# A convolution stage with eight row buffers, and weight sums moved from its first part into its second

## The reference, cut to what matters

```python
b_g, c_g, v = jnp.split(rmsnorm_and_modulate(x) @ w_in, 3, axis=-1)   # w_in: 1024 x 3072
u = c_g * v
z = causal_conv3_per_channel(u, conv_w)        # taps j = 0, 1, 2
out = (b_g * z) @ w_out                        # then x + (1 + g1) * out, norm, router, experts
```

## Time and profile before

| | us |
|---|---|
| median of 3 runs | 6204.08 (6202.45 to 6206.72) |
| the profiled execution's own time | 6206.02 |
| its span, first to last instruction | 6204.3 |
| conv front: PE's first and last product | 3204.0 to 3535.6 |
| conv second part: PE's first and last product | 3535.6 to 4233.1 |

### The profile page before, as it was taken

The page is one execution under the profiler, slowest core; times in us unless marked ns, Lnnn a source line. Parts: engine busy times, 40 slices in busy tenths (PEclk is TensorE's granted clock), DMA queues, the critical chain, the costliest instruction groups (busy, mean ns, idle before and its releaser), DMA issues. The chain is left out here.

```text
span 6204.3 us, 82965 instructions
## 1 busy us (share of the span) xinstructions
PE 5864.6 (95%) x28274; PEld 4784.7 (77%) x28275; DVE 3805.1 (61%) x5360; ACT 2134.5 (34%) x3188; POOL 2024.4 (33%) x1866
## 2 busy tenths in 40 slices
PE   7999989999899999999979999998997999999994
PEld 5876668888678888888867788887775888888884
DVE  6889945554455545555535588876776454556555
ACT  2334432222244334434334323321113333444434
POOL 6555538860122223222225500000112222222222
PEclk9999999999899999999989999999998999999997
DMA  4665664442267666777557845544445656777767
GB/s 152 176 189 153 191 222 151 139 137 82 105 213 214 195 179 196 220 209 220 156 152 268 290 145 182 185 148 160 154 156 186 192 170 174 216 219 238 214 201 282
DMA packets 620014, 1152.41 MB, mean 186 GB/s; under 512 B 121940, under 2 KB 218804, under 8 KB 618809
## 3 DMA queue, kind: packets, MB, share of 16 engines
q1 hardware_dynamic: 422256, 799.04, 38.0%
q0 software_dynamic: 92896, 315.82, 18.9%
q10 hardware_dynamic: 104682, 35.19, 2.2%
HBM read 863.32 MB, written 286.29 MB: 185 GB/s over the span
## 5 line engine op out<-in xcount | busy, mean ns | idle before, releaser
L2279 DVE SCALAR_TENSOR_TENSOR m_o<-m_pO,m_weight_of,m_gate 128x512 f32<-128x512 f32 x316 | 234.2, 746 | 711.3 <-PE m_pO L2022 397.3
L2246 DVE TENSOR_TENSOR m_w_lo<-m_w_raw,m_w_hi 128x1024 fp32r<-128x1024 f32 x512 | 596.1, 1214 | 0.1
L1906 POOL COPY m_gather_now<-m_gather_of 128x1 int32 (+1 forms) x161 | 181.6, 1128 | 1155.3 <-DMA x<-m_o,m_scatter_now 929.5
L2077 ACT ACTIVATE m_xT_hi<-m_pX 128x512 fp32r<-128x512 f32 x320 | 191.4, 599 | 999.8 <-PE m_pB L141 994.3
L139 PE MATMUL m_pA<-m_w_lo,m_xT_hi 128*128 128x512 f32 x1280 | 517.4, 404 | 14.7 <-DVE m_xT_lo L2257 14.7
L2065 ACT ACTIVATE m_w_hi<-m_w_raw 128x1024 fp32r<-128x1024 f32 x512 | 505.6, 1053 | 50.2 <-DMA m_w_raw<-in_moe_w_dram 28.9
L2018 PE MATMUL m_pO<-m_w_lo,m_hT_hi 128*128 128x512 f32 x1280 | 513.5, 401 | 0.4 <-ACT m_hT_hi L2082 0.2
L141 PE MATMUL m_pA<-m_w_hi,m_xT_hi 128*128 128x512 f32 x1280 | 503.3, 393 | 0.0
L140 PE MATMUL m_pA<-m_w_hi,m_xT_lo 128*128 128x512 f32 x1280 | 500.5, 391 | 0.0
L2018 PE MATMUL m_pO<-m_w_hi,m_hT_hi 128*128 128x512 f32 x1280 | 499.4, 390 | 0.0
L139 PE MATMUL m_pB<-m_w_lo,m_xT_hi 128*128 128x512 f32 x1280 | 498.1, 389 | 0.0
(11 more groups left out here) (524 smaller groups left out, 13561.0 us busy)
## 6 DMA issues: line engine op xcount, KB each, us to landing
m_w_raw<-in_moe_w_dram SPq DMA_DIRECT2D x384, 1024.0 KB, 7.2
conv_op_raw<-xr SPq DMA_DIRECT2D x84, 1024.0 KB, 5.2
glu_ada<-in_ada_w_dram POOLq DMA_DIRECT2D x96, 256.0 KB, 3.2
a_x<-in_x_dram SPq DMA_DIRECT2D x32, 512.0 KB, 3.6
a_ada<-in_ada_w_dram POOLq DMA_DIRECT2D x64, 256.0 KB, 3.5
s_u<-u SPq DMA_DIRECT2D x64, 256.0 KB, 2.7
s_r<-k SPq DMA_DIRECT2D x64, 256.0 KB
glu_x<-in_x_dram SPq DMA_DIRECT2D x32, 512.0 KB
```

The lines of the kernel that those rows point to most:

```text
L1906: pool.tensor_copy(gx[:], gidx[:, bass.ds(t, 1)]).then_inc(gi_ready, 1)
L2077: act.activation(xT_hi[:, 4 * q:4 * q + 4, :], pX[:, 4 * q:4 * q + 4, :], ACT.Copy).then_inc(xt_hi, 1)
L2246: tt(W13[s][1][:, m, k:k + 2, :], W13[s][0][:, m, k:k + 2, :], W13[s][2][:, m, k:k + 2, :].bitcast(F32), ALU.subtract).then_inc(w13_lo, 1)
L2279: dve.scalar_tensor_tensor(out=ob[:, n, :], in0=pO[:, n, :], scalar=wslot[:, bass.ds(tile_, 1)], in1=gate2[:, n, :], op0=ALU.mult, op1=ALU ...
```

## The change

- Eight row buffers. SP loads blocks 0 and 1 at once, and block b + 2 when block b has been turned. `std_of` of block b + 2 now stands at the head of ACT's round b, and `scaled` of block b + 2 in DVE's round b ahead of `taps_of(b, 1)`.
- POOL makes only the weight sums of quarter 1 in the front (two in block 0, one each in blocks 1 and 2). Those of quarters 2 and 3 become 24 small steps of 128 x 128 instructions (`small_mix`), two DMAs in and one out each, run in groups 0 to 2 and 4 to 6 of the second part: two ahead of a group's first stores of z and two behind them.
- The waits for the mix room move to the first instruction that writes each 8 KB of it: `keep` of operation 0 on ACT (tile 2), operations 1 and 3 on DVE (tiles 0 and 1). The places of `kept`, `vs`, `bs` change accordingly.
- Rows 4 to 6 take the place that weight 2 had, so weight 2 moves to a place that quarter 0's weights hold until the front's last product. SP loads it then, ahead of operand 2, and its split follows block 7.
- Low parts for `cout`: 0 between two sums of operation 81, 1 after it, 2 to 4 after 82, none after 83. The last three (`LATE_LOWS`) are made in `cout`, first of all on DVE, and PE waits for each at its first use.

```diff
-        mixes = [(MIXED, c, kk) for c in range(1, CHUNKS) for kk in range(KH)]
+        mixes = [(MIXED, 1, kk) for kk in range(KH)]
...
-            for _ in range(1 if b else 5):
+            for _ in range(2 if b == 0 else 1 if b < 3 else 0):
                 self.steps.append(mixes.pop(0))
...
+        self.small = [(c, kk, j) for c in range(2, CHUNKS) for kk in range(KH) for j in range(3)]
...
-        w_at = (48, 60, 136, 0, 12, 24, 36)
+        w_at = (48, 60, 12, 0, 24, 136, 36)
...
+        def all_mixed(eng, s):
+            eng.wait_ge(mix_st[s], 16 * len(range(s, len(seven.steps), TILES_)))
...
-                if kind == MIXED:
+                if kind == MIXED and c == 1:
                     mixed(sp, MIXED, c)
+                elif kind == MIXED:
+                    for q in range(2):
+                        sp.wait_ge(small_st[q], 16 * 3 * KH // 2 * (c - 1))
...
-            for j in range(TPB):
+            for j in range(2 * TPB):
                 sp.dma_start(rows[j][:], x_view[j]).then_inc(n_ld[j], 16)
...
-                if b + 1 < TB:
+                if b + 2 < TB:
                     sp.wait_ge(t_psum, KD * (b + 1))
                     for j in range(TPB):
-                        sp.dma_start(rows[j][:], x_view[TPB * (b + 1) + j]).then_inc(n_ld[j], 16)
+                        s = TPB * (b % 2) + j
+                        sp.dma_start(rows[s][:], x_view[TPB * (b + 2) + j]).then_inc(n_ld[s], 16)
...
-            for r in range(3):
+            for r in range(2):
                 weights(1, r)
...
             sp.wait_ge(mm, GROUPS * TB)
+            weights(1, 2)
             operand(2)
             weights(1, 3)
...
+                else:
+                    all_mixed(act, 2)
                 act.activation(kept[0][JS[i]][:], bank(n, JS[i])[:], ACT.Copy).then_inc(copied, 1)
...
             for b in range(TB):
+                if b + 2 < TB:
+                    for n in range(TPB * (b + 2), TPB * (b + 3)):
+                        std_of(n)
                 c_copy(b, 0)
...
-                if b + 2 < TB:
-                    for n in range(TPB * (b + 2), TPB * (b + 3)):
-                        std_of(n)
-            for s in range(TILES_):
-                act.wait_ge(mix_st[s], 16 * len(range(s, len(seven.steps), TILES_)))
+            w_high(1, 2)
...
-                ks = {OPS - 3: range(0, 3), OPS - 2: range(3, 6), OPS - 1: range(6, KD)}.get(n, ())
+                ks = {OPS - 3: range(0, 6), OPS - 2: range(6, KD)}.get(n, ())
...
+            def small_mix(i):
+                cc, kk, j = seven.small[i]
+                s, tt = i % 2, pool.tensor_tensor
+                if i + 1 < len(seven.small):
+                    small_fetch(i + 1)
+                pool.wait_ge(small_ld[s], 32 * (i // 2) + 32)
+                a11, a21, a12, a22 = (small[s][:, h, m * P:(m + 1) * P] for h in range(2) for m in range(2))
+                c(tt(a22, a21, a22, ALU.add))
+                c(tt(a21, a11, a21, ALU.subtract))
+                c(tt(a11, a22, a11, ALU.subtract))
+                c(tt(a12, a12, a11, ALU.subtract))
+                pool.dma_start(ws_dram[cc - 1, kk][:, :, j, :], small[s][:]).then_inc(small_st[s], 16)
...
             for n in range(TPB, 2 * TPB):
-                dve.wait_ge(t_psum, KD)
                 scaled(n)
...
-                taps_of(b, b % 2, 1, q(1))
-                gated(b, 1)
                 if b + 2 < TB:
                     for n in range(TPB * (b + 2), TPB * (b + 3)):
                         scaled(n)
+                taps_of(b, b % 2, 1, q(1))
+                gated(b, 1)
+            w_low(1, 2)
...
+                if n == 1:
+                    all_mixed(dve, 0)
+                if n == 3:
+                    all_mixed(dve, 1)
...
+                    if n == OPS - 3:
+                        next_low(0)
...
+            for k in range(KD if glu else KD - LATE_LOWS, KD):
+                dve.tensor_tensor(w_lo[:, k, :], w_raw[:, k, :], w_hi[:, k, :].bitcast(F32), ALU.subtract).then_inc(w_split, 1)
             dve.tensor_tensor(select[:], ident[:, 0:NL], ident[:, 64:64 + NL], ALU.add).then_inc(sel_set, 1)
```

More of the change, by code:

```diff
@@ L44 @@
 NG, EG, NE = 4, 8, 32
+KH = KD // 2
+SUPER = T // (2 * HALF)
+CHUNKS = 4
+SEVEN = 7
+LATE_LOWS = 3
 FE = 512
@@ L1280, in project @@
             _, here = core.sb_at(ctx, f"{tag}_w", [P, 22, D])
-            w_lo, w_hi, there, first_lo, first_hi = ready
+            w_raw, w_lo, w_hi, there, first_lo, first_hi = ready
             assert here == there
@@ L1669, in products @@
                             pe.wait_ge(w_split, (place * KD + k) // KQ + 1)
+                        if not glu and isinstance(i, int) and i + s + place == 0 and k >= KD - LATE_LOWS:
+                            pe.wait_ge(w_split, k - (KD - LATE_LOWS) + 1)
                         last = product(pe, pM[s][:, b, :], (h_hi[s][:, k, :], h_lo[s][:, k, :]),
@@ L2478, in conv_in @@
         w0_raw, w0_lo, w0_hi = first_w
-        rows = [at_(f"rows{j}", 48 + 4 * j, [P, D]) for j in range(TPB)]
+        last_row, last_row_at = core.sb_at(ctx, f"{tag}_rows7", [P, D])
+        rows = [at_(f"rows{j}", 48 + 4 * j, [P, D]) for j in range(TPB)] + [at_(f"rows{TPB + j}", 136 + 4 * j, [P, D]) for j in range(3)] + [last_row]
+        small = [nc.alloc_sbuf_tensor_at(f"{tag}_small{n}", [P, 2, W], F32, offset=last_row_at + 2 * KBYTES * n) for n in range(2)]
         junk = at_("junk", 64, [P, D])
@@ L2689, in turned @@
                 for j in range(TPB):
-                    last = pe.transpose(pT[n % 2][:, j * P:(j + 1) * P], rows[j][:, k * P:(k + 1) * P], ident[:])
+                    last = pe.transpose(pT[n % 2][:, j * P:(j + 1) * P], rows[TPB * (b % 2) + j][:, k * P:(k + 1) * P], ident[:])
                 last.then_inc(t_psum, 1)
@@ L2816, in store, with small_fetch @@
                 pool.dma_start(z_view[MC * (1 + g // SUPER) + m][2 * (g % SUPER) + t], z[q][:]).then_inc(y_st[q], 16)
-            for g in range(OPS // SEVEN):
-                store(g, 0)
-                store(g, 1)
+            def small_fetch(i):
+                cc, kk, j = seven.small[i]
+                s = i % 2
+                if i >= 2:
+                    pool.wait_ge(small_st[s], 16 * (i // 2))
+                for h in range(2):
+                    pool.dma_start(small[s][:, h, :], w_view[cc][:, KH * h + kk, j, :]).then_inc(small_ld[s], 16)
+            def small_mix(i):
+                cc, kk, j = seven.small[i]
+                s, tt = i % 2, pool.tensor_tensor
[8 more added lines that the diff above has]
+                pool.dma_start(ws_dram[cc - 1, kk][:, :, j, :], small[s][:]).then_inc(small_st[s], 16)
+            pool.wait_ge(t_psum, KD * TB)
+            small_fetch(0)
+            done = 0
+            for g in range(OPS // SEVEN):
+                for part in (2, 0, 1, 1):
+                    for _ in range(part if g % SUPER < 3 and g < 2 * SUPER else 0):
+                        small_mix(done)
+                        done += 1
+                    if part == 2:
+                        store(g, 0)
+                        store(g, 1)
                 if g + 1 < OPS // SEVEN:
@@ L3021, in program @@
         core.phase(project, ident, "cout", 1, False, zT, conv_w_out[0], rows(x1[0:T, :]), norm2_g,
-                moe_wg, moe_bg, moe_we, moe_be, mod, x1, hn, routes, slots[1], ready=(*ahead[1:], ahead_at, *n_src[1:]))
+                moe_wg, moe_bg, moe_we, moe_be, mod, x1, hn, routes, slots[1], ready=(*ahead, ahead_at, *n_src[1:]))
         core.phase(moe, ident, "m1", 1, routes, slots[1], table, *experts, final=(out, final_g.rearrange("(a d) -> a d", a=1)))
```

35 lines of the change are left out of this document (18 added, 17 removed).

## The result

The changed kernel took 6157.28 us (median of 4 executions, 6154.40 to 6161.72) where the kernel before took 6203.26 (4 executions): a ratio of 0.9926, 95% interval 0.9908 to 0.9943. Forecast were 6161 and a range of 6150 to 6179; faster, as the likeliest case said. The profiled execution of the changed kernel took 6154.4, span 6152.6, which is 51.7 less than before.

| stretch | before | after | gained |
|---|---|---|---|
| start to the first turning | 3200.4 | 3199.1 | 1.3 |
| front: first turning to the first pass of the second part | 335.2 | 295.3 | 39.9 |
| second part: first to last pass | 697.5 | 691.8 | 5.7 |
| last pass to the second tile of `cout` | 29.9 | 28.0 | 1.9 |
| from there to the end | 1941.3 | 1938.4 | 2.9 |

A forecast was written before the change was run, and what follows sets the result against it. PE, busy 95% of the span, was taken as the bound, so only its waits could pay. Gains of 37.5 + 4 + 1.4 = 43 us off the profiled 6206.0 gave 6163, a median of 6161, range 6150 to 6179.

The forecast's parts named there:

- likeliest case: Whole kernel: the forecast as summed, faster, with its own range of 6155 to 6169 us; chance 0.67.
- Front: First part of the stage: eight row buffers and the new order gain 37.5 us, from 28 to 40.
- the 40.3 of loss: Front, from block 1's rows being due: PE loses 40.3 us, 27.2 idle and 13.1 in slow passes.
- three small deductions: Front: losses taken off the gain, 1.3 us in block 0, 0.5 in the other blocks, 1.0 from loads at the start.
- only help: Front: POOL makes eight weight sums fewer there, said only to help; no size given.
- The rival in which late rows hold up `c_copy`: Front: ACT's norm jobs ahead of `c_copy` become the line, half the waits stay; gain 23 us, 6181; chance 0.12.
- Start of the second part: Waits at first use: operation 2's wait goes, operation 4 starts late; 8 us lost instead of 12.1, 4 gained.
- The roughly 2 us of slow passes: Start of the second part: slow passes of about 2 us expected behind the wait at operation 4.
- The issue of weight 2: SP's queue, ahead of operand 2: four added loads delay everything behind them by 3.4 to 6.5 us.
- Small sums: Second part: 24 steps on idle POOL, 1.8 us each, cost PE 0, covered by DVE's slack of 11.9 per group.
- The rival of a DVE that becomes the bound: Second part: small sums hold up DVE; at 5.4 us a step the kernel is slower by about 15, 6219; chance 0.05.
- End: Start of `cout`: fewer low parts ahead of the last sums, so the stage starts 1.4 us earlier; 1.4 gained.

The follow-up runs named there:

- rows_old: The changed kernel with four row buffers and the old order in the front, all else as changed: 6188.85 us, ratio to before 0.9974.
- front_only: The kernel before with only eight row buffers, their loads and the new places of `std_of` and `scaled`: 6172.05 us, ratio to before 0.9950.
- front_spread: The kernel before with the eight buffers and new order, and the front's twelve weight sums spread over the blocks: 6165.62 us, ratio 0.9941.
- jobs_late: The changed kernel with `std_of` back at the end of ACT's round and `scaled` back behind `gated(b, 1)` on DVE: 6186.56 us, ratio to before 0.9970.
- after_twin: The changed kernel again, unedited, timed beside the version with weight 2 loaded early: 6157.50 us, ratio to before 0.9929.
- lows_old: The changed kernel with all eight low parts for `cout` made before it, two of them in operation 83: 6165.61 us, ratio to before 0.9943.
- w2_early: The changed kernel with weight 2 at its old place, loaded in block 7, and the last high parts for `cout` an operation later: 6154.09 us.
- wait_first: The changed kernel with ACT again waiting for all stores of the sums ahead of operation 0: 6163.50 us, one execution.

## Why the prediction was right

**Front: 37.5 forecast, 39.9 measured.** The mechanism and the 40.3 of loss were right; all but 0.4 of it is gone. Of the seven waits besides the first, block 1's 9.07 came in the main from POOL's five sums in block 0 (rows_old), though the eight buffers cover most of that too (front_only). The three small deductions did not occur. *Block 0, 1.3*: eight norm jobs took 1.37 each, 10.9 in all where 12.6 were reckoned from the earlier trace rows, so `c_copy` came at 3230.09 and no copy was late. *Start loads, 1.0*: the first wait of PE is 26.3 against 26.2, and the first pass follows the first turning by 3.7 us, against 3.6. *Other blocks, 0.5*: no such wait.
One sentence was mis-sized: that eight sums fewer on POOL "only help". They are worth 4 us, since five sums in block 0 make the rows late where ACT has no cover (front_only and front_spread). The rival in which late rows hold up `c_copy` was thus real in this one block, and POOL's new order removed it.
In the account of the loss, the line was reckoned from the loads through the norm jobs to the scalings; jobs_late shows that the scalings stand behind the last gating, whenever the rows come, and that without the new place of the jobs 23.9 of the 39.9 are not had.

**Start of the second part: 4 forecast, 5.7 (and 7.4 in after_twin) measured.** That operation 4 decides, through SP's queue, was right. Its operand left at t = 27.2 (forecast 26.5 to 29.6) and PE started it at t = 39.1 (forecast 37.4 to 40.5), 6.4 late (forecast 4 to 7). The term failed in two pieces. The roughly 2 us of slow passes were added and did not come: behind the 3.37 the granted clock was 1.00. That was luck, since behind a wait of 2.51 at the same operation in lows_old it fell (last section). And the lateness was spread over operations 2, 3 and 4 (0.59, 1.69, 3.37); that weights 3 on ACT would hold up operation 3 was not foreseen. The issue of weight 2 was costed at 3.4 to 6.5 and took 1.96, while the four loads of weights 4 took 9.33. w2_early shows the whole of this loss to be the price of moving weight 2: without the move it is 0.

**Small sums: 0 forecast, 0 measured.** A step takes POOL 2.83 us, not 1.8, since its instructions take 0.46 with DVE idle and up to 1.86 beside it, 0.71 on average; and it takes DVE at most 0.52, where 1.8 was allowed for. The prediction took the rule of the Trainium skill, "SBUF — State Buffer", section "Who interferes with whom", that GpSimd and such DVE instructions shut each other out, to mean that DVE pays for every sum. But by that section the one that comes second waits, so POOL can pay too. The trace agrees with this: POOL's instructions stretched, and DVE paid at most a fifth of what POOL was busy, 4.65 against 25.5. The rival of a DVE that becomes the bound falls, up to three times the work.

**End: 1.4 forecast, 1.9 measured.** The second tile was still bound as forecast: DVE's first work for it, released by the constants, started at 4210.93, and PE's wait fell to 1.07 (forecast 0.1 to 1). lows_old bears 1.6 of it out.

**Sum.** 43 forecast; 47.5 in these three stretches. The median fell by 46.

## What to carry to other kernels

A wait for "rows" names the last piece of a chain, not the piece to move: more buffers gave 2 to 7 us, and placing the jobs ahead of work that itself waits for PE gave 24 to 29. When a load is moved to free its place, reckon what it pushes back in its queue to the last transfer that has a due time, and try the version that leaves it where it was. The small sums given to an idle POOL cost DVE little here; their due time at whoever loads their results is what to keep an eye on. The larger sums of the front were not as cheap: five of them at once made rows late, and scalings of 0.75 took 1.56 to 2.65 beside one.

## What the runs showed of the hardware

Waits of like length left different clocks behind them. Windows around a wait of 2.63 us in the front of rows_old, and around the wait of 3.37 at operation 4 of the changed kernel:

```profile
3295.00:3303.00 8.00, 5.44 (x25) 4.17 (x23) 7.59 (x9) 2.15 (x5) 6.65 (x6) 1.00 0.49 164
3303.00:3307.00 4.00, 3.92 (x16) 3.24 (x17) 1.14 (x3) 2.71 (x4) 3.68 (x5) 0.64 0.37 139
```

```profile
3525.00:3533.00 8.00, 5.12 (x23) 3.92 (x21) 6.38 (x7) 3.38 (x3) 1.52 (x3) 1.00 1.02 375
3533.00:3537.00 4.00, 3.51 (x15) 2.93 (x16) 4.00 (x5) 3.55 (x4) 0.00 (x0) 1.00 1.01 391
```

In the 8 us of the first window, which holds 2.56 of the wait's 2.63, PE was busy 5.44; in those of the second, which holds 2.88 of the 3.37, 5.12. Behind the wait the first case fell to a mean of 0.64, with passes at the level of 1.2 GHz among those at 2.4, and the second stayed at 1.00, the level of 2.4 GHz. In the first, turnings follow the wait, in the second, passes, but this does not tell them apart: behind another wait of 2.63 in the front of rows_old, with turnings behind it, the clock stayed at 1.00, and behind one of 2.51 at operation 4 of lows_old, with passes behind it, it fell to a mean of 0.63. The 4 us from the end of these two waits:

```profile
3384.44:3388.44 4.00, 4.00 (x22) 3.44 (x23) 1.19 (x2) 2.71 (x4) 1.85 (x2) 1.00 0.39 155
```

```profile
3538.54:3542.54 4.00, 4.00 (x12) 3.21 (x13) 4.00 (x5) 4.00 (x5) 0.07 (x1) 0.63 0.99 347
```

What does tell them apart stays open. A wait of 7.0 (wait_first) left 0.50.

The four loads of a weight took SP between 1.96 and 9.33 us to issue in the same kernel within 20 us.
